# Bands of exact entries for the pooling mixer, and a table of counts on VectorE for each mixed tile's first 16 columns

## The reference, cut to what matters

```python
POOL_WINDOWS = (2, 4, 8, 16)          # one window for each quarter (group) of the 2048 features
def multiscale_pool_mixer(h, pool_w, pool_scale):
    cs = jnp.cumsum(hf, axis=1)
    t = jnp.arange(S)
    for g, w in enumerate(POOL_WINDOWS):
        c = cs[..., sl]
        c_prev = jnp.pad(c, ((0, 0), (w, 0), (0, 0)))[:, :S]
        count = jnp.minimum(t + 1, w).astype(jnp.float32)[None, :, None]
        diff = (c - c_prev) / count - hf[..., sl]
        outs.append(jnp.einsum('bsc,cd->bsd', diff, pool_w[g]))
    return jnp.concatenate(outs, axis=-1) * pool_scale
x = x + multiscale_pool_mixer(rms_norm(x, pool_norm[l]), pool_w[l], pool_scale[l])
x = x + swiglu(rms_norm(x, ffn_norm[l]), w_gate[l], w_up[l], w_down[l])
```

## Time and profile before

| | |
|---|---|
| Time, median of 3 runs | 1771.49 us (1771.15 to 1771.55) |
| The profiled execution's own time | 1770.85 us |
| Its span, first to last instruction | 1769.1 us |
| TensorE busy | 1761.5 us, 100% of the span |
| VectorE busy | 1130.7 us, 64% |
| ScalarE busy | 914.3 us, 52% |
| GpSimd busy | 113.1 us, 6% |
| Granted TensorE clock, mean | 0.999 |

### The profile page before, as it was taken

One profiled execution on the slowest core, in us unless ns is written; L12 is line 12 of the kernel. 1 busy time (PEld: TensorE's weight loads), 2 busy tenths in 40 slices (PEclk: granted clock), 3 DMA queues, 4 the chain that ended last, 5 costly groups with the idle time before them and its releaser, 6 DMA issues.

```text
span 1769.1 us, 29325 instructions
## 1 busy us (share of the span) xinstructions
PE 1761.5 (100%) x10438; PEld 1564.0 (88%) x10438; DVE 1130.7 (64%) x1460; ACT 914.3 (52%) x1176; POOL 113.1 (6%) x132
## 2 busy tenths in 40 slices
PE   9999999999999999999999999999999999999998
PEld 6888888888888888889999888888888888888887
DVE  5766666556666666678997776666655566666554
ACT  6666664334444453456775466666533344445433
POOL 2100000000000001124111420000000000000000
PEclk9999999999999999999999999999999999999999
DMA  7555556545555566545445555555665455556642
GB/s 282 195 188 190 189 197 229 191 155 177 190 190 190 190 223 196 175 152 160 148 137 179 190 184 191 189 188 188 230 200 166 162 190 190 190 190 222 227 146 72
DMA packets 86017, 328.79 MB, mean 186 GB/s; under 512 B 9680, under 2 KB 11088, under 8 KB 85840
## 3 DMA queue, kind: packets, MB, share of 16 engines
q1 hardware_dynamic: 85680, 327.03, 55.5%
q10 hardware_dynamic: 288, 1.11, 0.2%
HBM read 326.01 MB, written 2.10 MB: 185 GB/s over the span
## 4 chain that ended last, share of the span: by engine, by line
PE 100%; DVE 0%; issue 0%; DVEq 0%; ACT 0%; POOL 0%; POOLq 0%
PE ps L435 58%; PE ps L436 31%; PE ps L505 2%; PE ps L443 1%; PE ps L445 1%; PE ps L444 1%; PE ps L799 1%; PE ps L798 1%; PE ps L797 1%; PE ps L633 0%; PE ps L632 0%; PE ps L631 0%; PE ps L685 0%; PE ps L493 0%; PE ps L705 0%; PE ps L706 0%
## 5 line engine op out<-in xcount | busy, mean ns | idle before, releaser
L1238 DVE TENSOR_TENSOR w_lo<-raw,w_hi 128x1024 fp32r<-128x1024 f32 (+2 forms) x564 | 736.0, 1308 | 419.1 <-ACT w_hi L850 416.9
L435 PE MATMUL ps<-xg,w_hi 128*128 128x512 f32 x2880 | 999.7, 390 | 0.0
L850 ACT ACTIVATE w_hi<-raw 128x1024 fp32r<-128x1024 f32 (+2 forms) x565 | 630.9, 1120 | 548.9 <-PE ps L436 533.2
L436 PE MATMUL ps<-xg,w_lo 128*128 128x256 f32 x2880 | 812.1, 282 | 0.0
L435 PEld LDWEIGHTS ps<-xg,w_hi 128*128 128x128 f32 x2880 | 540.5, 188 | 113.5 <-DVE w_lo L1238 0.3
L436 PEld LDWEIGHTS ps<-xg,w_lo 128*128 128x128 f32 x2880 | 544.3, 189 | 0.1
L435 PE MATMUL ps<-act,w_hi 128*128 128x512 f32 x1320 | 458.0, 390 | 0.0
L436 PE MATMUL ps<-act,w_lo 128*128 128x256 f32 x1320 | 372.2, 282 | 0.0
L435 PEld LDWEIGHTS ps<-act,w_hi 128*128 128x128 f32 x1320 | 247.7, 188 | 51.9
L436 PEld LDWEIGHTS ps<-act,w_lo 128*128 128x128 f32 x1320 | 249.5, 189 | 0.0
L1318 DVE TENSOR_TENSOR sums<-ps,cross 128x512 f32<-128x512 f32 x88 | 60.8, 691 | 93.1 <-ACT cross L928 93.1
(11 more groups left out here) (200 smaller groups left out, 1240.2 us busy)
## 6 DMA issues: line engine op xcount, KB each, us to landing
raw<-w_gate SPq DMA_DIRECT2D x176, 512.0 KB, 3.2
raw<-w_up SPq DMA_DIRECT2D x176, 512.0 KB, 3.2
raw<-w_down SPq DMA_DIRECT2D x120, 704.0 KB, 4.2
raw<-w_o SPq DMA_DIRECT2D x32, 512.0 KB, 3.2
raw<-w_last SPq DMA_DIRECT2D x11, 512.0 KB, 3.2
raw<-w_q_a SPq DMA_DIRECT2D x8, 512.0 KB, 3.2
raw<-w_kv_a SPq DMA_DIRECT2D x8, 512.0 KB, 3.3
raw<-w_q_nope SPq DMA_DIRECT2D x8, 512.0 KB, 3.2
```

Of the source, the lines that this page charges most:

```text
L435: pe.matmul(ps[:, bank, :], w_hi[:, s, j * P:(j + 1) * P], moving, start=start, stop=False)
L436: return pe.matmul(ps[:, bank, 0:SEQ], w_lo[:, s, j * P:(j + 1) * P], moving[:, 0:SEQ], start=False, stop=stop)
L850: nc.scalar.activation(dst, src, ACT.Copy).then_inc(hi_ready, 1)
L1238: nc.vector.tensor_tensor(lo, src, hi.bitcast(F32), ALU.subtract).then_inc(lo_ready, 1)
```

## The change

The band keeps only entries that are exact in fp32r: 1/w, a power of two, in place of 1/count, with the diagonal reduced by count/w in place of one. What is then wrong in the first 16 columns is a factor for each column, w/count; VectorE multiplies the 16 columns of each mixed tile by it, in place in PSUM, ahead of `pool_out`. The table of factors (four groups by 16 columns) is appended to the constants. The constants' load is waited for before the first tile is mixed, and no longer ahead of the rotary angles. The fifth matmul of a tile, the stored low part and GpSimd's work for it are gone.

```diff
-C_COLS = C_SIGN + 1
+C_FEW = C_SIGN + 1
+C_COLS = C_FEW + GROUPS * PAD
-B_FIRST, B_SECOND, B_LOW, B_COLS = 0, SEQ, SEQ + P, SEQ + P + PAD
+B_FIRST, B_SECOND, B_COLS = 0, SEQ, SEQ + P
...
-                    pe.matmul(ps[:, bank, 0:PAD], first_hi, band[:, g, B_LOW:B_LOW + PAD], start=False, stop=False)
...
-            pe.wait_ge(band_ready, 3)
+            pe.wait_ge(band_ready, 2)
             mix(0)
             pool_product(3, 0)
-            pe.wait_ge(band_ready, 6)
+            pe.wait_ge(band_ready, 4)
             mix(1)
...
             def pool_out(t):
                 ve.wait_ge(mixed, t + 1)
+                few = ps[:, mix_bank(t), 0:PAD]
+                step(nc.vector.tensor_tensor(few, few, const[:, C_FEW + t // GT * PAD:C_FEW + (t // GT + 1) * PAD],
+                                             ALU.mult))
                 nc.vector.scalar_tensor_tensor(x[:, t, :], ps[:, mix_bank(t), 0:SEQ], gain[:, G_SCALE + t, :],
                                                x[:, t, :], ALU.mult, ALU.add).then_inc(evacuated, 1)
 
             product_lo(0)
             product_lo(1)
+            ve.wait_ge(const_landed, 16)
...
             ffn(0, 0, 2, None)
             ve.wait_ge(pos_landed, 16)
-            ve.wait_ge(const_landed, 16)
             rope_angles()
...
-                gp.wait_ge(band_ready, 3 * k + 2)
-                nc.gpsimd.tensor_tensor(band[:, groups, B_LOW:B_LOW + PAD], band_in[:, groups, 0:PAD],
-                                        band[:, groups, B_FIRST:B_FIRST + PAD].bitcast(F32),
-                                        ALU.subtract).then_inc(band_ready, 1)
...
+    for g, w in enumerate(WINDOWS):
+        c[:, C_FEW + g * PAD:C_FEW + (g + 1) * PAD] = w / np.minimum(np.arange(PAD) + 1.0, w)
...
-        out[:, g, 0:SPILL] = np.where(seen, 1.0 / np.minimum(t + 1.0, w), 0.0) - own
+        out[:, g, 0:SPILL] = np.where(seen, 1.0 / w, 0.0) - own * np.minimum(t + 1.0, w) / w
```

## The result

The changed kernel takes 1773.92 us (median of 22 runs, 1773.45 to 1774.70), the one before 1771.30 us (median of 22, 1770.85 to 1772.25): 2.6 us more. The ratio is 1.0015, with a 95% interval of 1.0009 to 1.0021. It is slower, and by less than the 0.2% that I had set as the bound of "no change". 1774.1 was forecast.

A forecast was written before the change was run, and what follows sets the result against it. TensorE is busy nearly throughout, but VectorE's list was taken to decide its load at 53.13 us. Group 0's 0.18 plus 3 x 0.79 made 2.55 us; 1771.5 + 2.6 gave 1774.1 us, range 1773.6 to 1774.6.

The forecast's parts named there:

- The place: TensorE's first load of chunk 4, at 53.13 us: work added to VectorE's list arrives there, TensorE's saved 1.8 us doesn't.
- e = 0.205: Cost in us of each of VectorE's 16 multiplications: about 0.167 for the instruction and 0.035 waiting for its end.
- Rival A: Between multiplication and `pool_out`: writing PSUM and reading it back is dear, 1775.9 us at 0.32 us each; chance 0.15.
- rival C: On VectorE: the new instruction is hidden, its cost near the lower bound of 0.09 us, 1772.2 us; chance 0.05.
- The sum: Shift at the end of VectorE's fourth split (48.68 us): 0.18 + 3 x 0.79 = 2.55 us.
- Group 0: First four tiles: VectorE replaces TensorE in setting the pace, first tile ready 0.11 earlier, last `pool_out` 0.18 us later.
- Groups 1 to 3: The later tiles, paced by VectorE: 0.82 us added to each group, of which 0.79 arrives.
- the slack of 0.03 on ScalarE: ScalarE's `gained` behind each `pool_out`: 0.03 us slower than VectorE, so 0.79 of 0.82 us arrives per group.
- TensorE's waits: TensorE meets the delay early, in waits up to chunk 4: saved 1.8 and added 2.6 us together, not added to the shift.
- B: At chunk 4's low part, if not tied to VectorE's list: TensorE keeps its saving, 1769.5 us; chance 0.05.
- D: TensorE's waits between 42 and 56 us make its clock fall: 3.5 us more, 1777.6 us; chance 0.03.
- At nothing: Counted as free: the constants' wait (landed at 22.4, asked at about 26.7 us), GpSimd's two subtractions, loads of weights.

The follow-up runs named there:

- e1: The changed kernel with the fifth matmul of each mixed tile kept: 1774.17 us.
- e2: The changed kernel without VectorE's multiplications: 1771.05 us.
- e3: The changed kernel with a second multiplication, by a table of ones, behind each first one: 1777.50 us.
- e9: The changed kernel with the multiplication of the next tile issued ahead of each `pool_out`: 1772.30 us.
- e8: The changed kernel without VectorE's multiplications and without GpSimd's wait for the four splits ahead of tile 10: 1771.25 us.
- e10: The changed kernel without VectorE's multiplications, with ScalarE making chunk 4's high part ahead of its squares of tiles 14 and 15: 1771.28 us.
- e11: The kernel before the change, with ScalarE making chunk 4's high part ahead of its squares of tiles 14 and 15: 1771.76 us.
- e5: The kernel before the change, without GpSimd's wait for the four splits ahead of tile 10: 1771.80 us.
- e4: The changed kernel without GpSimd's wait for the four splits ahead of tile 10: 1773.11 us.

## Why the prediction was right

- **The place.** One wait of 0.26 us was taken for the meeting of two chains, and the chain through VectorE's list, GpSimd's additions, ScalarE's squares and the fifth split was followed back. After the change every one of these links lies 2.95 us later. Shown by the trace after, by e1, e2 and e3: VectorE's work counts in full, and of TensorE's 1.8 us only 0.1 with the multiplications in (e1) and 0.46 without them (e2), both by way of VectorE's pace in group 0.
- **The price.** e = 0.205 was worked out from instructions of one column, and of 128 and 256; it came out at 0.21 (0.17 + 0.04). Rival A, a dear write to PSUM, is out: nothing like 0.267 was seen. That the wait is the larger part is shown by e9, and rival C's bound of 0.09 for an unwaited one was met there as 0.08. The prediction sets its rows against the Trainium skill, VectorE: DVE Perf Modes, "The DRAIN you can't avoid". It read that section too widely: the section also says that a next instruction that is not held starts earlier, and the 0.08 agrees with that. What these runs contradict is that the wait between two instructions costs nothing: here it costs 0.13.
- **The sum.** Forecast 2.55, in the trace 2.84 at chunk 4, in the medians 2.62. That the medians came so near is in part luck: the stage was forecast 0.29 too short, and the 0.2 us that came back at the very end was not forecast at all. Two terms of the stage were off. Group 0: +0.18 forecast, 28.85 - 28.43 less the 0.11 of a later start = 0.31 measured. I gave the first tile 0.11 us for TensorE's being done earlier, but VectorE was still at `product_lo` (24.07 + 2.73 = 26.80, and the first `pool_out` starts at 26.73), so VectorE could not begin earlier and nothing came of it. Groups 1 to 3: 0.79 each forecast, 0.83 to 0.85 measured; the slack of 0.03 on ScalarE that I took off was none.
- **TensorE's waits.** Forecast in their order about 0, 0.8, 1, 0.9 and 1.6 us; measured 0.26, 0.85, 1.02, 0.87 and 1.67. All but the second hold 0.04 that lies behind such a load without a wait, too.
- **The rivals.** B (TensorE keeps its saving) fell with e1 and e2, and e8, e10 and e11 add that it could not have kept it even with this link cut: in the kernel before, the sum of squares is ready only 0.55 us ahead of TensorE, and the low part of chunk 3 1.5 us (48.68, 50.14). D (the clock falls) did not come with the change: 4.7 us of waits between 41 and 56 us left the clock at 1.00. It did come in e3, with 3.4 us of waits between 42 and 47 us, and even there it cost nothing that I can find in the time, as TensorE was not the last to be ready.
- **At nothing.** The constants landed at 9.9 + 12.4 = 22.3 us, 4.5 us before VectorE's first multiplication.

What the runs don't settle: e2 is 0.2 us below before and its trace 0.46; the difference is within the spread of the executions. Why VectorE's last scalings follow closer on each other in every kernel with multiplications is open as well.

## What to carry to other kernels

An engine that is busy for all of the span need not be the one that decides in the stage that a change touches. Look for its shortest waits on others: a wait of a quarter of a microsecond is the place where a second chain arrives at the same time, and work that is moved onto that chain is paid in full, while what the busy engine saves becomes waiting. A short instruction in place in PSUM costs mostly the wait for its own end; issue something else between it and its reader, and more than half of the price is gone (1.70 of 2.84 us in e9). And before a wait is taken out as needless, look at what would then run beside it.

## What the runs showed of the hardware that I had not expected

- VectorE and GpSimd slow one another a great deal when VectorE reads two SBUF tensors: four `gained` 3.14 us in place of 1.66 (e5), two GpSimd additions 2.42 in place of 1.55 (e10). Either can be the one that loses: in e4 a split keeps its 1.21 and the addition beside it takes 1.85 in place of 0.74. A `pool_out`, with one tensor in PSUM, keeps its pace (e4).
- The clock fell from 2.4 to 1.2 GHz for about three microseconds behind waits of 1.57, 1.50 and 0.30 us that followed closely on each other (e3), while five waits with one of 1.67 us, farther apart, left it (after). That the distance between the waits decides is not shown.
- The stage starts between 24.07 and 25.25 us (the first `product_lo` in twelve traces). In some traces TensorE waits for the first pool weights (1.9 us in e8, which starts last); in e3 and e5 it hardly does, and its weight loads at about 6 us take 0.34 us in place of 0.19. From chunk 4's first load to the end it is 1717.5 to 1717.8 us in all but e10 and e11. So most of the spread of a run's time is likely to lie in that start, though no kernel was traced twice, and a shift of 0.2 us is better read in a trace, from a mark behind it.
